# A norm's sums of squares as one row on TensorE instead of as columns

## The chip, the core and the metric

The kernel runs on one core of one Trainium2 chip. The core has five engines that matter here: TensorE (PE, with its weight loads shown apart as PEld), VectorE (DVE), ScalarE (ACT), GpSimd (POOL) and SyncE (SP), which issues most transfers. The metric is the device time of one execution in microseconds.

## The reference, cut to what matters

Four layers over a sequence of 256 tokens with 1024 features, batch 1: two with four mixers side by side, one hybrid, one of retention. Each layer has a mixer half and a feed-forward half. Each half begins with a norm of x; in the first two layers each half also ends with a norm of its output y:

```
def rms_norm(x, gain=None):
    y = xf * lax.rsqrt(jnp.mean(xf * xf, axis=-1, keepdims=True) + RMS_EPS)
...
h = rms_norm(x, norm_g[l, 0]) * (1.0 + sc1) + sh1
y = mixer_block(h, ...)
x = x + gt1 * rms_norm(y, norm_g[l, 1])
h = rms_norm(x, norm_g[l, 2]) * (1.0 + sc2) + sh2
y = jnp.square(jax.nn.relu(h @ w_up[l])) @ w_down[l]
x = x + gt2 * rms_norm(y, norm_g[l, 3])
```

In layers 2 and 3 the update is `x = x + gt * y` with no norm of y. So there are 8 norms of x and 4 norms of y, 12 in all.

## The kernel before

x is held transposed in SBUF, features on partitions: `X` is 128 x 8 x 256 (8 tiles `k` of 128 features, 256 tokens). The sum of squares of a token thus runs over partitions, and PE makes it: `unit_sums` (L586). The 8 tiles are grouped in five units, `UNITS = ((0, 1), (2, 3), (4, 5), (6,), (7,))`.

A norm of x (`norm_of`, L603) goes so. ACT squares a unit (L626) into one of two buffers `sq`, so that the Square of unit u waits until PE has summed unit u-2. PE multiplies the squares by a column of ones (L591). After the last unit ACT takes the root from PSUM (L629), DVE the reciprocal (L637), and `spread` (L599) lets PE broadcast the two columns `r` over all partitions as the row block `R` in PSUM. Then DVE multiplies a tile of X by R (L641), ACT adds the shift and rounds to `hi` (L632), DVE makes the remainder `lo` (L645), tile by tile, and the next projection (`gemm_phase`, L519) starts on the first tile of `hi`.

Weights come through a ring of six slots by DMA. Each slot is split by ACT into a rounded part (L411) and by DVE into a remainder (L417); PE multiplies three products of the parts. A slot is 48 matmul records of 128x256. The first slot of a phase is split ahead of the norm (`PRE = 1`), the second after it, since ACT and DVE run their instructions in the order of the code.

A norm of y stands in `rows_gemm_phase`. The last weight slot finishes the output tiles in the order of k. As each unit ends, ACT squares it from PSUM (L820) and takes a gated copy (L822), and PE puts the sums of a unit behind the multiplications (L789) of the next. Then follow root (L825), reciprocal (L844) and spread (L599), and DVE updates X unit by unit (L851, L853), which releases the Squares of the norm of x that follows. The order on each engine is that of the code, with semaphores between engines. A table load of ACT stands before the root where its last function was of another table.

A matmul with f32 operands shows as two records in the trace, each with its weight load. So a tile's two products with the column of ones are four records, each with a load of 128 columns of weights and one moving column.

Of the kernel before, what the change touches and what calls it, by code (L numbers as in the profile page):

```python
# [13 lines left out]
P = 128  # L14
SEQ = 256
# [230 lines left out]
def build(nc, stream, small, const, rows, x_in, pos_in, out, SM, CT):  # L246
    with ExitStack() as ctx:
# [42 lines left out]
        def cst(name):  # L290
            c, _, w = CT[name]
            return constS[:, c:c + w]
# [293 lines left out]
        def unit_sums(pe, u, sq, bank, ready, done):  # L586

            pe.wait_ge(*ready.at(u + 1))
            for c in range(len(UNITS[u])):
                for m in range(TT):  # L590
                    mm = pe.matmul(PS[:, bank, m:m + 1], sq[:, u % 2, c * SEQ + m * P:c * SEQ + (m + 1) * P], ones[:, 0:1],  # L591
                                   start=u + c + m == 0, stop=u == len(UNITS) - 1, skip_group_check=True)
            mm.then_inc(*done.one())

        def spread(pe, r, bank, ready, done):

            pe.wait_ge(*ready.at(1))
            for m in range(TT):
                mm = pe.matmul(PS[:, bank, m * P:(m + 1) * P], r[:, m:m + 1].to_broadcast((P, P)), ident, start=m == 0,  # L599
                               stop=True, skip_group_check=True)  # L600
            mm.then_inc(*done.one())

        def norm_of(l, half, updated):  # L603
# [3 lines left out]
            sq = area(TEMP_AT, 2, 512)  # L607
            tmp, r = spare[:, 0:1024].rearrange("p (i t) -> p i t", i=4), stat[:, 48:50]
            R = PS[:, 2, 0:SEQ]
            xsq, xsum, xrt, xr, rx, td, hd, ld = (sig(n) for n in (  # L610
                "x_squares", "x_square_sums", "x_roots", "x_rstd", "x_rstd_spread", "x_scaled", "h_hi_ready", "h_lo_ready"))
            state["h_hi"] = [hd.at(k + 1) for k in range(KD)]
            state["h_lo"] = [ld.at(k + 1) for k in range(KD)]

            def pe_part(pe):
                for u in range(len(UNITS)):
                    unit_sums(pe, u, sq, 0, xsq, xsum)
                spread(pe, r, 2, xr, rx)

            def act_part(act):  # L620
# [7 lines left out]
                act.wait_ge(*xsum.at(len(UNITS)))  # L628
                act.activation(r, PS[:, 0, 0:TT], ACT.Sqrt, bias=cst("eps"), scale=1.0 / D).then_inc(*xrt.one())  # L629
                for k in range(KD):  # L630
# [4 lines left out]
            def dve_part(dve):  # L635
                dve.wait_ge(*xrt.at(1))
                dve.reciprocal(r, r).then_inc(*xr.one())  # L637
                dve.wait_ge(*rx.at(1))
# [103 lines left out]
        def rows_gemm_phase(blk, name, l, lhs, half, acts_split=0, acts_ready=None, next_norm=None):  # L742
# [6 lines left out]
            gate = mod_part(l, half, 2)  # L749
            bd, ysq, ysum, yrt, yr, ry, yg, yt, xu = (sig(n) for n in (  # L750
                "tile_products", "y_squares", "y_square_sums", "y_roots", "y_rstd", "y_rstd_spread", "y_gated", "y_scaled", "x_updated"))
            following = slots_to_split() if next_norm else []
            norm = norm_of(*next_norm, xu) if next_norm else None
            sq, T, z = area(TEMP_AT, 2, 512), area(TEMP_AT + 1024, 2, 512), area(0, KD, SEQ)
            r, R = stat[:, 50:52], PS[:, 3, 0:SEQ]
            last, n_units = len(slots) - 1, len(UNITS)
# [17 lines left out]
            def _(pe):  # L774
# [23 lines left out]
                if normed:  # L798
                    unit_sums(pe, n_units - 1, sq, 0, ysq, ysum)
                    spread(pe, r, 3, yr, ry)  # L800
                if norm:
# [9 lines left out]
            def _(act):  # L811
                for n in slots[split_before:] + following:
                    split_hi(act, n)
                if normed:
# [9 lines left out]
                    act.wait_ge(*ysum.at(n_units))  # L824
                    act.activation(r, PS[:, 0, 0:TT], ACT.Sqrt, bias=cst("eps"), scale=1.0 / D).then_inc(*yrt.one())  # L825
                if norm:
# [3 lines left out]
            def _(dve):  # L830
# [11 lines left out]
                if normed:  # L842
                    dve.wait_ge(*yrt.at(1))
                    dve.reciprocal(r, r).then_inc(*yr.one())  # L844
                    dve.wait_ge(*ry.at(1))
# [95 lines left out]
        def short_mixers(l, convT, lqT, lkT, lrT, LV, LG, MU, MV, oT):  # L941
# [29 lines left out]
                "square_sums", "mean_ready", "root_ready", "outputs_ready", "outputs_turned", "gla_zeroed"))  # L971
            dfr, vn, wm, gt = sig("centred"), sig("gmlp_normed"), sig("ws_masked"), sig("gla_out_taken")
            c4 = c.rearrange("p (n t) -> p n t", n=4)
# [207 lines left out]
        def nsa_phase(l, kvcT, QK, VN, oT, S):  # L1181
# [21 lines left out]
            cs, sd, ex, pc = sig("cmp_scores"), sig("cmp_shifted"), sig("cmp_exp"), sig("cmp_probs")  # L1203
            pct, pcs, oc, oct_ = (sig(n) for n in ("cmp_probs_T", "cmp_probs_T_taken", "cmp_out", "cmp_out_taken"))
            ws, wt, mxd, pe_, ptp, pts, ob, obt = (sig(n) for n in (
                "scores_in_psum", "scores_taken", "row_max", "probs_ready", "probs_T_in_psum", "probs_T_taken",
                "attn_out", "attn_out_taken"))
            gd, fin, ft = sig("gates_ready"), sig("outputs_ready"), sig("outputs_turned")
# [403 lines left out]
        def delta_inputs(Q, AB):  # L1612
# [6 lines left out]
            taken = sig("gemm_bank_taken")  # L1619
            tap0, cv, sl, sqd, ss, rt, nr = (sig(n) for n in (  # L1620
                "first_tap", "conv_done", "conv_silu", "squares_ready", "l2_sums", "root_ready", "l2_done"))
            ga, ge, gl, bt = sig("gate_abs"), sig("gate_exp"), sig("gate_log"), sig("beta_ready")
# [569 lines left out]
```

## Time and profile before

| what | us |
|---|---|
| median of 3 runs | 1766.13 |
| lowest and highest of them | 1761.39, 1768.34 |
| the profiled execution's own time | 1766.4 |
| its span (first to last instruction) | 1764.4 |
| PE busy | 1561.6 |
| DVE busy | 1077.8 |
| ACT busy | 716.1 |

The span lies 2.0 us below the execution's own time. The mean granted TensorE clock over the span is 0.909 of full speed. A row of a timeline merges neighbouring instructions of one kind: it gives the start from the start of the span, the length, the engine, the line, what is written and read, the shape and the number of records, and in brackets how long the engine had been idle and who ended that. PEclk is the granted share of the TensorE clock: 1.00 is 2.4 GHz, 0.50 is 1.2 GHz.

### The profile page before, as it was taken

How to read it: one execution, taken by the hardware profiler on the slowest of the kernel's cores; microseconds unless marked ns; L12 is line 12 of the kernel's file. 1: busy time of each engine (PE TensorE's matmuls, PEld its weight loads, DVE VectorE, ACT ScalarE, POOL GpSimd, SP SyncE). 2: the span in 40 equal slices, each digit the busy share in tenths (PEclk: the TensorE clock that was granted, in tenths of full speed). 3: DMA queues.
4: the chain of work that ended last, by engine and by line, in shares of the span. 5: the costliest groups of instructions: out<-in, count | busy, mean ns of one | idle time of the engine just before them, and what ended most of it. 6: DMA issues, size and time to landing. Idle time of an engine off the chain costs nothing. (4 is left out here: it accounts for less than half of the span.)

```text
span 1764.4 us, 27370 instructions
## 1 busy us (share of the span) xinstructions
PE 1561.6 (89%) x11950; PEld 1506.8 (85%) x11950; DVE 1077.8 (61%) x1279; ACT 716.1 (41%) x797; POOL 277.4 (16%) x221
## 2 busy tenths in 40 slices
PE   2897689999898689999897685999989998899999
PEld 2886589999787589999897584999989997899998
DVE  6765757787455448688474633576895443456444
ACT  2533345433542445533474411433334443343332
POOL 0000200053000001044000111010253700300012
PEclk7998779999798579999798885899998999889999
DMA  9570549787140228888243001378893542436650
GB/s 395 224 262 1 207 187 350 291 332 291 72 160 32 76 92 320 324 308 333 99 170 117 1 1 35 146 281 303 312 354 144 189 173 93 143 129 229 217 211 29
DMA packets 47207, 336.71 MB, mean 191 GB/s; under 512 B 5360, under 2 KB 5744, under 8 KB 6768
## 3 DMA queue, kind: packets, MB, share of 16 engines
q1 hardware_dynamic: 46224, 333.09, 50.7%
q8 instruction: 94, 1.54, 0.3%
q10 hardware_dynamic: 864, 1.87, 0.3%
q14 instruction: 25, 0.20, 0.0%
HBM read 333.89 MB, written 1.05 MB: 190 GB/s over the span
## 5 line engine op out<-in xcount | busy, mean ns | idle before, releaser
L417 DVE TENSOR_TENSOR weights_hi_lo<-ring,weights_hi_lo 128x2048 fp32r<-128x2048 f32 x213 | 514.5, 2417 | 399.2 <-ACT weights_hi_lo L411 398.4
L411 ACT ACTIVATE weights_hi_lo<-ring 128x2048 fp32r<-128x2048 f32 x213 | 407.4, 1914 | 638.8 <-PE PS L519 347.1
L519 PE MATMUL PS<-hi,weights_hi_lo 128*128 128x256 f32 x3200 | 526.9, 288 | 25.5 <-DVE weights_hi_lo L417 17.1
L519 PEld LDWEIGHTS PS<-hi,weights_hi_lo 128*128 128x128 f32 x3200 | 451.3, 195 | 29.4 <-DVE weights_hi_lo L417 19.1
L789 PE MATMUL PS<-acts_hi_lo,weights_hi_lo 128*128 128x256 f32 x3552 | 446.3, 288 | 33.9 <-DVE weights_hi_lo L417 21.1
L789 PEld LDWEIGHTS PS<-acts_hi_lo,weights_hi_lo 128*128 128x128 f32 x3552 | 439.2, 196 | 41.3 <-DVE weights_hi_lo L417 25.0
L519 PE MATMUL PS<-lo,weights_hi_lo 128*128 128x256 f32 x1600 | 326.7, 286 | 0.0
L519 PEld LDWEIGHTS PS<-lo,weights_hi_lo 128*128 128x128 f32 x1600 | 253.8, 195 | 0.0
L428 DVE CUSTOM_DVE_ANT_0 ring<-ring,cond 128x1024 f32<-128x1024 f32 x192 | 248.4, 1333 | 1.0 <-DMA smallS<-in_small_dram 0.9
L737 POOL CAST acts_hi_lo<-arena 128x512 fp32r<-128x512 f32 x74 | 73.8, 998 | 993.6 <-PE PS L789 538.2
L519 PE MATMUL PS<-weights_hi_lo,hi 128*128 128x256 f32 x1248 | 203.2, 284 | 9.2 <-DVE weights_hi_lo L417 8.0
L519 PEld LDWEIGHTS PS<-weights_hi_lo,hi 128*128 128x128 f32 x1248 | 172.8, 190 | 12.0 <-DVE weights_hi_lo L417 9.0
L739 POOL TENSOR_TENSOR acts_hi_lo<-arena,acts_hi_lo 128x512 fp32r<-128x512 f32 x74 | 130.2, 1760 | 5.9
L519 PE MATMUL PS<-weights_hi_lo,lo 128*128 128x256 f32 x624 | 125.8, 283 | 0.0
L519 PEld LDWEIGHTS PS<-weights_hi_lo,lo 128*128 128x128 f32 x624 | 96.8, 189 | 0.0
L591 PEld LDWEIGHTS PS<-constS,arena 128*128 128x128 f32 x384 | 63.4, 256 | 23.1 <-ACT arena L626 22.2
L591 PE MATMUL PS<-constS,arena 128*128 128x1 f32 x384 | 64.0, 294 | 20.8 <-ACT arena L626 19.9
L400 PE MATMUL PS<-constS,arena 128*128 128x128 f32 x120 | 21.0, 338 | 37.0 <-DVE arena L1551 11.2
L400 PEld LDWEIGHTS PS<-constS,arena 128*128 128x128 f32 x120 | 17.8, 177 | 39.6 <-DVE arena L1551 11.4
L632 ACT ACTIVATE hi<-spare,mods 128x256 fp32r<-128x256 f32 x64 | 31.7, 506 | 31.8 <-DVE spare L641 31.8
L626 ACT ACTIVATE arena<-X 128x512 f32<-128x512 f32 (+1 forms) x40 | 21.7, 544 | 47.4 <-PE PS L591 18.7
L1955 POOL TENSOR_TENSOR arena<-arena,constS 128x1024 f32<-128x1024 f32 x6 | 11.9, 2000 | 181.4 <-DVE arena L1880 172.6
(325 smaller groups left out, 1100.4 us busy)
## 6 DMA issues: line engine op xcount, KB each, us to landing
ring<-in_stream_dram SPq DMA_DIRECT2D x313, 1024.0 KB, 4.9
constS<-in_const_dram SPq DMA_DIRECT2D x1, 1856.0 KB, 11.3
cond<-in_rows_dram SPq DMA_DIRECT2D x2, 512.0 KB, 6.0
arena<-in_x_dram ACTq DMA_DIRECT2D x1, 1024.0 KB, 12.5
smallS<-in_small_dram SPq DMA_DIRECT2D x1, 883.0 KB, 12.4
out_dram<-arena ACTq DMA_DIRECT2D x2, 256.0 KB, 2.5
out_dram<-arena SPq DMA_DIRECT2D x2, 256.0 KB, 2.9
constS<-in_const_dram SPq DMA_DIRECT2D x1, 320.0 KB, 13.0
```

The source lines that it names most:

```text
L400: mm = pe.transpose(PS[:, bank0 + i // 4, i % 4 * P:(i % 4 + 1) * P], src_of(i), ident)
L411: act.activation(wsp[:, g % 2, 0, :], ring[:, n % RING, :], ACT.Copy).then_inc(*hi_ready.one())
L417: dve.tensor_tensor(wsp[:, g % 2, 1, :], ring[:, n % RING, :], wsp[:, g % 2, 0, :].bitcast(F32), ALU.subtract).then_inc(used["dve"], 1)
L428: ins = dve.tensor_tensor_reduce(w[:, r, :], w[:, r, :], cond[:, 0 if q < 12 else 1, :], 1.0, 0.0, ALU.mult, ALU.add, mods[:, q, k:k + 1])
L519: mm = pe.matmul(o, lhs, rhs, start=k + g + j == 0, stop=k == KD - 1 and j == 2, skip_group_check=True)
L591: mm = pe.matmul(PS[:, bank, m:m + 1], sq[:, u % 2, c * SEQ + m * P:c * SEQ + (m + 1) * P], ones[:, 0:1], start=u + c + m == 0, stop=u == ...
L626: act.activation(sq[:, u % 2, 0:len(tiles) * SEQ], X[:, tiles[0]:tiles[-1] + 1, :].rearrange("p k t -> p (k t)"), ACT.Square).then_inc(*xs ...
L632: act.activation(hi[:, k, :], tmp[:, k % 4, :], ACT.Identity, bias=mods[:, q, k:k + 1]).then_inc(*hd.one())
L737: pool.tensor_copy(asp[:, a % 2, 0, :, :], src).then_inc(*acts_hi.one())
L739: pool.tensor_tensor(asp[:, a % 2, 1, :, :], src, asp[:, a % 2, 0, :, :].bitcast(F32), ALU.subtract).then_inc(*acts_lo.one())
L789: mm = pe.matmul(y_of(k), w[:, g, k * P:(k + 1) * P], x[:, g, :], start=i + g + j == 0 and (k % 2 == 0 or k == KD - 1), stop=i == last and ...
L1955: pool.tensor_tensor(CT[v % 2], LT, cst(f"level{v}").unsqueeze(1).broadcast_to((P, 8, P)), ALU.mult).then_inc(*ctd.one())
```

## The change

The squares become the moving operand and one column of ones the stationary one. A tile needs one matmul in place of two, with a single output partition: the sums of all 256 tokens form one row in PSUM. ACT takes the root of that row, 1x256 in place of 128x2, into a row of SBUF (`root`). Then PE turns the row into two columns with two matmuls of one contraction row each (new, in `spread`), and DVE takes the reciprocal of the columns from PSUM in place of SBUF. From there all is as before. A wait is added on PE (for the root) and the wait of the reciprocal is now for PE, not for ACT. All 12 norms use it. The rest of the diff drops names of semaphores that nothing used.

```diff
@@ -587,13 +587,17 @@
 
             pe.wait_ge(*ready.at(u + 1))
             for c in range(len(UNITS[u])):
-                for m in range(TT):
-                    mm = pe.matmul(PS[:, bank, m:m + 1], sq[:, u % 2, c * SEQ + m * P:c * SEQ + (m + 1) * P], ones[:, 0:1],
-                                   start=u + c + m == 0, stop=u == len(UNITS) - 1, skip_group_check=True)
+                mm = pe.matmul(PS[0:1, bank, 0:SEQ], ones[:, 0:1], sq[:, u % 2, c * SEQ:(c + 1) * SEQ],
+                               start=u + c == 0, stop=u == len(UNITS) - 1, skip_group_check=True)
             mm.then_inc(*done.one())
 
-        def spread(pe, r, bank, ready, done):
-
+        def spread(pe, root, r, bank, rooted, turned, ready, done):
+
+            pe.wait_ge(*rooted.at(1))
+            for m in range(TT):
+                mm = pe.matmul(PS[:, bank, SEQ + m:SEQ + m + 1], root[0:1, m * P:(m + 1) * P], ones[0:1, 0:1], start=m == 0, stop=True,
+                               skip_group_check=True)
+            mm.then_inc(*turned.one())
             pe.wait_ge(*ready.at(1))
             for m in range(TT):
                 mm = pe.matmul(PS[:, bank, m * P:(m + 1) * P], r[:, m:m + 1].to_broadcast((P, P)), ident, start=m == 0,
@@ -605,17 +609,17 @@
 
             q = mod_part(l, half, 0)
             sq = area(TEMP_AT, 2, 512)
-            tmp, r = spare[:, 0:1024].rearrange("p (i t) -> p i t", i=4), stat[:, 48:50]
+            tmp, r, root = spare[:, 0:1024].rearrange("p (i t) -> p i t", i=4), stat[:, 48:50], spare[0:1, 1024:1280]
             R = PS[:, 2, 0:SEQ]
-            xsq, xsum, xrt, xr, rx, td, hd, ld = (sig(n) for n in (
-                "x_squares", "x_square_sums", "x_roots", "x_rstd", "x_rstd_spread", "x_scaled", "h_hi_ready", "h_lo_ready"))
+            xsq, xsum, xrt, xc, xr, rx, td, hd, ld = (sig(n) for n in (
+                "x_squares", "x_square_sums", "x_roots", "x_roots_turned", "x_rstd", "x_rstd_spread", "x_scaled", "h_hi_ready", "h_lo_ready"))
             state["h_hi"] = [hd.at(k + 1) for k in range(KD)]
             state["h_lo"] = [ld.at(k + 1) for k in range(KD)]
 
             def pe_part(pe):
                 for u in range(len(UNITS)):
                     unit_sums(pe, u, sq, 0, xsq, xsum)
-                spread(pe, r, 2, xr, rx)
+                spread(pe, root, r, 2, xrt, xc, xr, rx)
 
             def act_part(act):
                 for u, tiles in enumerate(UNITS):
@@ -626,15 +630,15 @@
                     act.activation(sq[:, u % 2, 0:len(tiles) * SEQ],
                                    X[:, tiles[0]:tiles[-1] + 1, :].rearrange("p k t -> p (k t)"), ACT.Square).then_inc(*xsq.one())
                 act.wait_ge(*xsum.at(len(UNITS)))
-                act.activation(r, PS[:, 0, 0:TT], ACT.Sqrt, bias=cst("eps"), scale=1.0 / D).then_inc(*xrt.one())
+                act.activation(root, PS[0:1, 0, 0:SEQ], ACT.Sqrt, bias=cst("eps")[0:1], scale=1.0 / D).then_inc(*xrt.one())
                 for k in range(KD):
                     act.wait_ge(*td.at(k + 1))
                     act.activation(hi[:, k, :], tmp[:, k % 4, :], ACT.Identity,
                                    bias=mods[:, q, k:k + 1]).then_inc(*hd.one())
 
             def dve_part(dve):
-                dve.wait_ge(*xrt.at(1))
-                dve.reciprocal(r, r).then_inc(*xr.one())
+                dve.wait_ge(*xc.at(1))
+                dve.reciprocal(r, PS[:, 2, SEQ:SEQ + TT]).then_inc(*xr.one())
                 dve.wait_ge(*rx.at(1))
                 for k in range(KD + 1):
                     if k < KD:
@@ -747,12 +751,12 @@
             slots, todo = slots_of(name)
             normed = l < 2
             gate = mod_part(l, half, 2)
-            bd, ysq, ysum, yrt, yr, ry, yg, yt, xu = (sig(n) for n in (
-                "tile_products", "y_squares", "y_square_sums", "y_roots", "y_rstd", "y_rstd_spread", "y_gated", "y_scaled", "x_updated"))
+            bd, ysq, ysum, yrt, yc, yr, ry, yg, yt, xu = (sig(n) for n in (
+                "tile_products", "y_squares", "y_square_sums", "y_roots", "y_roots_turned", "y_rstd", "y_rstd_spread", "y_gated", "y_scaled", "x_updated"))
             following = slots_to_split() if next_norm else []
             norm = norm_of(*next_norm, xu) if next_norm else None
             sq, T, z = area(TEMP_AT, 2, 512), area(TEMP_AT + 1024, 2, 512), area(0, KD, SEQ)
-            r, R = stat[:, 50:52], PS[:, 3, 0:SEQ]
+            r, R, root = stat[:, 50:52], PS[:, 3, 0:SEQ], spare[0:1, 1280:1536]
             last, n_units = len(slots) - 1, len(UNITS)
             unit_ends = {tiles[-1]: u for u, tiles in enumerate(UNITS)}
 
@@ -797,7 +801,7 @@
                     mm.then_inc(*multiplied.one())
                 if normed:
                     unit_sums(pe, n_units - 1, sq, 0, ysq, ysum)
-                    spread(pe, r, 3, yr, ry)
+                    spread(pe, root, r, 3, yrt, yc, yr, ry)
                 if norm:
                     norm[0](pe)
 
@@ -822,7 +826,7 @@
                             ins = act.activation(z[:, k, :], y_of(k), ACT.Copy, scale=mods[:, gate, k:k + 1])
                         ins.then_inc(*yg.one())
                     act.wait_ge(*ysum.at(n_units))
-                    act.activation(r, PS[:, 0, 0:TT], ACT.Sqrt, bias=cst("eps"), scale=1.0 / D).then_inc(*yrt.one())
+                    act.activation(root, PS[0:1, 0, 0:SEQ], ACT.Sqrt, bias=cst("eps")[0:1], scale=1.0 / D).then_inc(*yrt.one())
                 if norm:
                     norm[1](act)
 
@@ -840,8 +844,8 @@
                 for n in following:
                     split_lo(dve, n)
                 if normed:
-                    dve.wait_ge(*yrt.at(1))
-                    dve.reciprocal(r, r).then_inc(*yr.one())
+                    dve.wait_ge(*yc.at(1))
+                    dve.reciprocal(r, PS[:, 3, SEQ:SEQ + TT]).then_inc(*yr.one())
                     dve.wait_ge(*ry.at(1))
                 for u, tiles in enumerate(UNITS):
                     n, ks = len(tiles), slice(tiles[0], tiles[-1] + 1)
...
```

PE at the end of the first y norm and the start of the x norm behind it (`y_squares`, `y_rstd` and `x_squares` are the semaphores waited for; L789 is the projection's own matmul), before:

```order
L591 MATMUL PS<-constS,arena 128x1 [waits y_squares]
L591 MATMUL PS<-constS,arena 128x1 x3
L789 MATMUL PS<-acts_hi_lo,weights_hi_lo 128x256 x6
L591 MATMUL PS<-constS,arena 128x1 [waits y_squares]
L591 MATMUL PS<-constS,arena 128x1
L591 MATMUL PS<-constS,arena 128x1 [waits y_squares]
L591 MATMUL PS<-constS,arena 128x1
L599 MATMUL PS<-constS,stat 128x128 [waits y_rstd]
L599 MATMUL PS<-constS,stat 128x128
L591 MATMUL PS<-constS,arena 128x1 [waits x_squares]
```

The same place on PE after the change (L590 are the sums, L598 the new turn, L603 the spread, L793 the projection):

```order
L590 MATMUL PS<-arena,constS 1x256 [waits y_squares]
L590 MATMUL PS<-arena,constS 1x256
L793 MATMUL PS<-acts_hi_lo,weights_hi_lo 128x256 x6
L590 MATMUL PS<-arena,constS 1x256 [waits y_squares] x2
L598 MATMUL PS<-constS,spare 128x1 [waits y_roots]
L598 MATMUL PS<-constS,spare 128x1
L603 MATMUL PS<-constS,stat 128x128 [waits y_rstd]
L603 MATMUL PS<-constS,stat 128x128
L590 MATMUL PS<-arena,constS 1x256 [waits x_squares]
```

Half as many matmuls make the sums, at the same places between the projection's, and two more stand between the root and the spread. On ACT and DVE no instruction is added, removed or moved; the root's shape and the reciprocal's source change. DVE at the same place, before and after:

```order
L417 TENSOR_TENSOR weights_hi_lo<-ring,weights_hi_lo 128x2048 [waits hi_ready]
L844 RECIPROCAL stat<-stat 128x2 [waits y_roots]
L851 TENSOR_TENSOR arena<-arena,PS 128x512 [waits y_gated,y_rstd_spread]
L853 TENSOR_TENSOR X<-X,arena 128x512 [waits y_scaled]
L851 TENSOR_TENSOR arena<-arena,PS 128x512 [waits y_gated]
```

```order
L417 TENSOR_TENSOR weights_hi_lo<-ring,weights_hi_lo 128x2048 [waits hi_ready]
L848 RECIPROCAL stat<-PS 128x2 [waits y_roots_turned]
L855 TENSOR_TENSOR arena<-arena,PS 128x512 [waits y_gated,y_rstd_spread]
L857 TENSOR_TENSOR X<-X,arena 128x512 [waits y_scaled]
L855 TENSOR_TENSOR arena<-arena,PS 128x512 [waits y_gated]
```

Nothing changes places there; the reciprocal waits one engine later.

## Rows read from the trace of the kernel before

**Rows 1.** The page's first line

```profile
span 1764.4 us, 27370 instructions
```

**Rows 2.** The chain that ended last, 1558 to 1695: start us, us, what

```profile
1558.26 2.90 PE PS L591 x24
...
1562.76 0.27 ACT stat L629
...
1563.27 1.24 PE PS L599 x4
...
1572.79 2.30 DVE weights_hi_lo L417
...
1575.13 119.88 PE PS L519 x1008
```

**Rows 3.** Timeline, 438 to 451: start us, us, instruction [idle before <-releaser]

```profile
438.79 0.26 ACT L825 ACTIVATE stat<-PS,constS 128x2 f32<-128x2 f32 x1 [0.33 <-PE PS L591]
...
440.05 0.69 DVE L851 TENSOR_TENSOR arena<-arena,PS 128x512 f32<-128x512 f32 x1 [0.80 <-PE PS L599]
...
442.18 6.98 PE L591 MATMUL PS<-constS,arena 128*128 128x1 f32 x32 [2.17 <-ACT arena L626]
...
445.27 0.42 DVE L853 TENSOR_TENSOR X<-X,arena 128x256 f32<-128x256 f32 x1
...
447.55 0.42 ACT L626 ACTIVATE arena<-X 128x256 f32<-128x256 f32 x1 [1.29 <-PE PS L591]
449.20 0.26 ACT L629 ACTIVATE stat<-PS,constS 128x2 f32<-128x2 f32 x1 [1.23 <-PE PS L591]
...
449.71 1.23 PE L599 MATMUL PS<-constS,stat 128*128 128x128 f32 x4 [0.55 <-DVE stat L637]
450.98 0.87 DVE L641 SCALAR_TENSOR_TENSOR spare<-X,mods,PS 128x256 f32<-128x256 f32 x2 [1.32 <-PE PS L599]
```

**Rows 4.** Windows: stretch, length, busy by engine, PEclk, DMA share, GB/s

```profile
33.00:40.20 7.20, 6.99 (x32) 6.90 (x32) 1.96 (x1) 3.32 (x6) 0.00 (x0) 0.50 1.01 420
43.10:49.30 6.20, 6.11 (x28) 6.14 (x29) 5.68 (x14) 4.26 (x8) 0.28 (x1) 0.50 0.75 302
...
442.10:449.20 7.10, 6.98 (x32) 6.90 (x32) 3.49 (x7) 2.12 (x6) 0.00 (x0) 0.50 0.00 1
452.10:455.60 3.50, 3.46 (x16) 3.49 (x17) 3.50 (x10) 2.11 (x5) 0.00 (x0) 0.51 0.00 0
...
143.20:148.30 5.10, 5.09 (x24) 4.23 (x25) 3.45 (x14) 0.11 (x1) 0.00 (x0) 0.50 0.01 3
1121.70:1124.60 2.90, 2.82 (x25) 2.82 (x25) 1.71 (x5) 1.71 (x4) 0.00 (x0) 0.99 0.79 322
```

**Rows 5.** Timeline of PE at 1484, dense f32 records of 512 columns

```profile
1484.50 10.46 PE L2085 MATMUL PS<-arena 128*128 128x512 f32 x24
```

**Rows 6.** Timeline of PE at 187, dense f32 records of 512 columns

```profile
187.51 3.78 PE L1464 MATMUL PS<-spare,constS 128*128 128x512 f32 x4 [2.98 <-DVE spare L1470]
```

**Rows 7.** Groups by form: count | busy us, mean ns | idle before

```profile
L645 DVE SCALAR_TENSOR_TENSOR lo<-spare,mods,hi 128x256 fp32r<-128x256 f32 x64 | 30.8, 481 | 2.9 <-ACT hi L632 2.9
L641 DVE SCALAR_TENSOR_TENSOR spare<-X,mods,PS 128x256 f32<-128x256 f32 x64 | 29.8, 476 | 10.5 <-PE PS L599 10.5
...
L1330 PE MATMUL PS<-ring,spare 128*32 128x128 f32 x128 | 18.3, 317 | 4.6 <-DVE spare L1227 4.6
...
L822 ACT ACTIVATE arena<-PS,mods 128x256 f32<-128x256 f32 x32 | 13.8, 473 | 0.0
...
L820 ACT ACTIVATE arena<-PS 128x256 f32<-128x256 f32 x8 | 3.1, 384 | 4.5 <-PE PS L789 4.5
...
L629 ACT ACT_TABLE_LOAD x2 | 2.6, 1283 | 0.0
```

**Rows 8.** Timeline at 849, DVE after a y norm's spread

```profile
849.51 0.69 DVE L851 TENSOR_TENSOR arena<-arena,PS 128x512 f32<-128x512 f32 x1 [1.31 <-PE PS L599]
```

**Rows 9.** Timeline at 1126, ACT at an x norm's root

```profile
1126.43 0.26 ACT L629 ACTIVATE stat<-PS,constS 128x2 f32<-128x2 f32 x1 [1.23 <-PE PS L591]
```

More of the change, by code:

```diff
@@ L971, in short_mixers @@
                 "square_sums", "mean_ready", "root_ready", "outputs_ready", "outputs_turned", "gla_zeroed"))
-            dfr, vn, wm, gt = sig("centred"), sig("gmlp_normed"), sig("ws_masked"), sig("gla_out_taken")
+            dfr, vn, wm = sig("centred"), sig("gmlp_normed"), sig("ws_masked")
             c4 = c.rearrange("p (n t) -> p n t", n=4)
@@ L1203, in nsa_phase @@
             cs, sd, ex, pc = sig("cmp_scores"), sig("cmp_shifted"), sig("cmp_exp"), sig("cmp_probs")
[L1204 to L1207, printed above, removed]
+            pct, pcs, oc = (sig(n) for n in ("cmp_probs_T", "cmp_probs_T_taken", "cmp_out"))
+            ws, wt, mxd, pe_, ptp, pts, ob = (sig(n) for n in (
+                "scores_in_psum", "scores_taken", "row_max", "probs_ready", "probs_T_in_psum", "probs_T_taken", "attn_out"))
             gd, fin, ft = sig("gates_ready"), sig("outputs_ready"), sig("outputs_turned")
@@ L1619, in delta_inputs @@
             taken = sig("gemm_bank_taken")
-            tap0, cv, sl, sqd, ss, rt, nr = (sig(n) for n in (
-                "first_tap", "conv_done", "conv_silu", "squares_ready", "l2_sums", "root_ready", "l2_done"))
+            tap0, cv, sl, sqd, ss, rt = (sig(n) for n in (
+                "first_tap", "conv_done", "conv_silu", "squares_ready", "l2_sums", "root_ready"))
             ga, ge, gl, bt = sig("gate_abs"), sig("gate_exp"), sig("gate_log"), sig("beta_ready")
```

## The prediction, made before the kernel ran

> **What bounds the kernel now.** I read the page first for the span [rows 1], then the chain that ended last, then a timeline of one norm, then windows for the granted clock. The chain is to be read from the bottom: nearly all of it is PE in the projections (119.88 us in one piece), and the pieces between are norms, in which it goes from engine to engine: PE's sums, the root 0.27, the spread 1.24, then DVE and ACT tile by tile and the split of the second weight slot on DVE, 2.30, before PE runs on [rows 2]. So a norm is serial and PE has nothing else to do in it; what a norm grows by, the span grows by, as long as PE is the bound behind it. I take that for all 12 norms.
>
> The timeline shows what a norm waits for [rows 3]. At 442.18 PE begins the sums of the x norm and is busy with them without a hole for 6.98 us, to 449.2. DVE has updated the last tile of X at 445.7, so for 3.5 us the sums alone hold the norm: ACT's Squares wait for PE (1.29 us before the last). Then the root comes 1.23 us after the last Square, the spread takes 1.32 us of DVE's time, and the projection starts. The windows say why the sums are slow: PEclk is 0.50 all through them, in this norm as in the first [rows 4]. At 1121.7 PE comes straight from a projection, at 2.4 GHz, and 25 of the same records take 2.82 us, 0.113 each, against 6.98/32 = 0.218.
>
> **The change, part by part.** Durations are from the profiled execution, 1766.4 us with a span of 1764.4, 0.3 us above the median of the runs shown.
>
> The sums. Before, a tile is four records, 0.87 us at 1.2 GHz and 0.45 at 2.4. After, it is one matmul with 256 moving columns, two records. Dense f32 records of 512 columns take (10.46 - 0.16)/24 = 0.429 us at 2.4 GHz [rows 5] and (3.78 - 0.2)/4 = 0.90 at 1.2 [rows 6], where I took off the last record's tail; half of that for 256 columns, twice for a tile: 0.43 and at most 0.90. So half as many matmuls are no less work: the weight load of 128 columns that paced a record is replaced by a stream of 256. At an equal clock the sums save (0.45 - 0.43) x 8 = 0.15 us in a norm of y, whose sums run at 2.4 GHz on PE's own path, 0.6 in four; in an x norm at 1.2 GHz I take nothing (0.87 against 0.85 to 0.90).
>
> The root. It reads 1x256 in place of 128x2. It is 0.26 now [rows 3]; ACT from PSUM with 256 columns and an operand of one column is 0.473, without that operand 0.384 [rows 7]. I take 0.47, since the root has such an operand: +0.21, bounds +0.12 and +0.25. That 127 partitions are left out saves nothing that a row shows. The Trainium skill (ScalarE: Activation LUTs, Rules for kernel authors) puts an instruction with a pointer bias at about 0.3 us plus 0.83 ns an element, an estimate of 0.51; by that the 12 roots cost 0.5 us more than by the row.
>
> The turn. Two matmuls, four records with one moving column, stand between root and reciprocal, with a hop on each side. The nearest row is the last unit's sums, the same four records between two ACT instructions: 1.23 us at 1.2 GHz [rows 3]. At 2.4 GHz it is the spread, 0.80 [rows 3], whose records have 128 moving columns. The hop from ACT to DVE falls away, 0.03. The reciprocal now reads PSUM: DVE with a PSUM operand takes 476 ns and without one 481 [rows 7], so nothing, at most 0.1. PE has nothing queued behind its new wait that could run before the spread, and DVE and ACT wait for that anyway: nothing covers the turn.
>
> So the fixed price of a norm is 0.21 + 1.23 - 0.03 = 1.41 us at 1.2 GHz and 0.21 + 0.80 - 0.03 = 0.98 at 2.4.
>
> The clock. This decides the rest. Through 7 us of records with one moving column, PE busy throughout, the clock stays at 0.50 [rows 4]. In projections behind a norm, records with 256 moving columns, it rises: 3.5 us after the start at 452.1 and 6.2 after that at 43.1, the shortest and longest of four such starts [rows 4]. It also rose 5.1 us into records whose stationary operand has only 32 columns, with 128 moving ones [rows 4, 7]. The new sums have one stationary column, fewer than any row, but stream 256 moving ones without a hole. I take it that they bring the clock up as the projections do.
>
> Then an x norm behind a y norm gains (6.98 - 3.5)/2 = 1.7 us at best and (6.98 - 6.2)/2 = 0.4 at worst in its sums, 1.1 in the middle; less 0.3, because at 2.4 GHz a Square that waits for PE (two buffers) leaves PE waiting in turn. I take 0.8. The turn and the spread follow within 3 us at 2.4 GHz: the spread's 1.32 becomes 0.80. Such a norm: 0.98 - 0.52 - 0.8 = -0.34, four of them -1.4. The first norm also has these sums, but a table load of 1.28 us [rows 7] stands behind its last Square and covers the end of them; I take 0. Two x norms of layers 2 and 3 come warm from a projection and lose the clock in the sums (1.23 us after the last Square, [rows 9], about 0.45 too much); if it holds: 0.98 - 0.52 - 0.45 = 0. The third has a table load there, which hid the sums: 0.98 - 0.52 = +0.46. The norms of y pay 0.98 x 4 = 3.9, less 0.6 for the sums; two of them had their spread at 1.2 GHz, as [rows 8], and I let one of these keep the clock: -0.5. Together +2.8.
>
> Nothing comes back at the start of the projection: the chain goes there over DVE to the second slot's split, not over PE's first slot [rows 2].
>
> The sum: -1.4 + 0 + 0 + 0.5 + 2.8 = +1.9, so 1768.3 us for the profiled kind of run, 1768 for the median.
>
> **The rivals.** (1) The new sums don't raise the clock. One stationary column of 128 may be too little work to count, and no row goes below 32. Then every x norm pays 1.41 (11.3 for eight), the y norms two at 0.98 and two at 1.41 less 0.6 (4.2): +15.5, 1782 us. Its place is the stretch from the first Square to the root; it decides wherever PEclk is 0.50 in the L590 stretch. The Trainium skill (TensorE: Matmul & The Clock Gate, Why this matters for your kernels) advises to keep TensorE busy continuously to reach the higher clock. By that the old sums, busy for 6.98 us, would have reached it too and the change could bring none: 12 x 0.98 - 0.6 = +11.2. The trace disagrees, 0.50 all through, so this reading gets no chance of its own.
>
> (2) The clock never falls between the y norm and the x norm, or is back at once. Then the x sums follow the Squares: the last tile of X at 445.7, its Square 0.12 later, 0.42 long, its sum 0.65 behind: 446.9 against 449.2, so 2.3 us a norm in place of 0.8, 6 us more in four, some 2 in the first norm: 1760 us. For it speaks that the y sums now stream too. Against it, PE does little from 438.8 to 442.2 but the spread, and will do little more [rows 3].
>
> (3) Small records don't run dense: the one-column weight load and a 256-column stream might leave holes of 0.1 us a record. 16 records in 12 norms would be up to 19 us where PE is the bound, some 12. The records with a 32-column load took 18.3 us for 128 of them, 0.14 each over both clocks [rows 7], with no hole of that kind, so I give this little; it ends near rival 1.
>
> **How the numbers follow.** The forecast has 0.66, its own range 1760 to 1775, since the clock's rise moves by 2.7 us between the rows and eight norms share it. Rival 1 has 0.23, rival 2 0.07, rival 3 0.04. A measurement of this kernel tells some 0.5% from no change, 8.8 us: faster is below 1757.3, slower above 1775. Faster gets 0.06 (most of rival 2 stays within), slower 0.27 (rivals 1 and 3), the same 0.67. The range for 8 in 10 takes in rival 1's middle: 1759 to 1783.
>
> **What would show it.** The L590 stretch of an x norm (32 records before, 16 after): PEclk well above 0.50 and 4.5 to 6.5 us long where I am right; 0.50 and 7 us in rival 1; under 5 with PEclk near 1 in rival 2. The root: 0.47 against 0.26. The gap of the reciprocal behind the root: 0.8 or 1.23. The spread's wait on DVE: 0.80 more often than 1.3. In the y norm's last slot the L590 records are 0.215 apart. I am wrong if the sums run at 1.2 GHz, or if the turn takes much more than 1.2 us.

## The result, and the profile after

| | median us (runs) | lowest to highest | profiled span | mean granted clock |
|---|---|---|---|---|
| before | 1764.71 (10) | 1760.09 to 1771.69 | 1764.4 | 0.909 |
| after | 1775.74 (10) | 1765.79 to 1782.22 | 1779.9 | 0.922 |

The ratio is 1.005, 95% between 1.0027 and 1.0072: some 8.8 us slower, and the whole interval lies above 1; the medians themselves lie 11.0 apart. The forecast was +1.9. The median after lies 0.7 us above the forecast's own range of 1760 to 1775 and inside its wider one of 1759 to 1783. The clock is higher on the mean, and the time is longer all the same; that is what has to be explained.

First the x norm of the forecast's rows, in the timeline (start us, us, instruction, idle before and releaser). They answer to [rows 3].

```profile
447.80 6.41 PE L590 MATMUL PS<-arena,constS 128*1 128x256 f32 x16 [2.17 <-ACT arena L630]
...
453.15 0.42 ACT L630 ACTIVATE arena<-X 128x256 f32<-128x256 f32 x1 [1.26 <-PE PS L590]
...
454.24 0.47 ACT L633 ACTIVATE spare<-PS,constS 1x256 f32<-1x256 f32 x1 [0.68 <-PE PS L590]
...
454.76 0.60 PE L598 MATMUL PS<-constS,spare 1*128 1x1 f32 x4 [0.56 <-ACT spare L633]
...
455.40 0.17 DVE L641 RECIPROCAL stat<-PS 128x2 f32<-128x2 f32 x1 [4.09 <-PE PS L598]
...
455.63 0.71 PE L603 MATMUL PS<-constS,stat 128*128 128x128 f32 x4 [0.26 <-DVE stat L641]
456.38 0.87 DVE L645 SCALAR_TENSOR_TENSOR spare<-X,mods,PS 128x256 f32<-128x256 f32 x2 [0.80 <-PE PS L603]
```

The sums take 6.41 us against 6.98, the root comes 0.68 us after the last Square against 1.23, the root is 0.47 against 0.26, the reciprocal starts 0.69 us after the root's end (454.71 to 455.40) against 0.03, and DVE waits 0.80 for the spread against 1.32. All of that was forecast, and the windows show why it is so: the clock rises in the sums. The columns are those of [rows 4]: the first norm, the x norm above, one that comes warm from a projection, where before the clock fell on the way [rows 9].

```profile
31.50:39.20 7.70, 5.52 (x16) 1.51 (x16) 2.78 (x5) 4.60 (x7) 0.00 (x0) 1.00 1.02 422
...
447.80:454.20 6.40, 6.27 (x16) 1.63 (x16) 3.41 (x7) 2.09 (x4) 0.00 (x0) 0.60 0.00 0
...
1131.90:1136.00 4.10, 3.85 (x16) 1.09 (x16) 1.68 (x5) 2.13 (x5) 0.00 (x0) 1.00 0.60 248
```

The 1.00 of the first row can't be taken as it stands. The first eight records of these sums (from 32.89 us) last 0.58 to 0.63 us and start 0.43 apart, twice the 0.22 of the later ones, which last 0.38: this is the pace of 1.2 GHz, whatever PEclk says there. The faster pace begins at about 36.5. So in the first norm, too, the clock rose within the sums.

The chain that ended last shows the same route as [rows 2], from the root over the turn and DVE to the split of the second weight slot (L417) and only then to PE:

```profile
1576.42 0.47 ACT spare L633
...
1576.94 0.61 PE PS L598 x4
...
1577.80 0.72 PE PS L603 x4
...
1586.80 2.30 DVE weights_hi_lo L417
...
1589.15 10.92 PE PS L519 x77
```

**Missed, first place: the sums inside the last weight slot of a y norm.** Here is PE's timeline there, first before, then after.

```profile
429.00 3.13 PE L789 MATMUL PS<-acts_hi_lo,weights_hi_lo 128*128 128x256 f32 x24 [0.38 <-DVE weights_hi_lo L417]
...
434.29 0.95 PE L591 MATMUL PS<-constS,arena 128*128 128x1 f32 x8
435.11 0.96 PE L789 MATMUL PS<-acts_hi_lo,weights_hi_lo 128*128 128x256 f32 x6
435.90 0.95 PE L591 MATMUL PS<-constS,arena 128*128 128x1 f32 x8
```

```profile
433.00 3.14 PE L793 MATMUL PS<-acts_hi_lo,weights_hi_lo 128*128 128x256 f32 x24 [0.39 <-DVE weights_hi_lo L417]
...
438.64 1.02 PE L590 MATMUL PS<-arena,constS 128*1 128x256 f32 x4
439.60 0.97 PE L793 MATMUL PS<-acts_hi_lo,weights_hi_lo 128*128 128x256 f32 x6
440.50 1.02 PE L590 MATMUL PS<-arena,constS 128*1 128x256 f32 x4
```

From one start of the sums to the next it is 434.29 to 435.90 = 1.61 us before and 438.64 to 440.50 = 1.86 after, with six records of the projection in both. From the slot's start to the root it is 438.79 - 429.00 = 9.79 before, and 443.54 - 433.00 = 10.54 after. In the weight loads' own rows an idle stretch stands before the first load of each return to the projection:

```profile
439.60 0.77 PEld L793 LDWEIGHTS PS<-acts_hi_lo,weights_hi_lo 128*128 128x128 f32 x6 [0.44 <-issue]
```

**Missed, second place: the second weight slot behind a norm.** PE's timeline at the third norm from the end, the last records of the first slot and the first of the second, before and after:

```profile
1137.28 0.40 PE L519 MATMUL PS<-lo,weights_hi_lo 128*128 128x256 f32 x2
1138.80 0.74 PE L519 MATMUL PS<-hi,weights_hi_lo 128*128 128x256 f32 x4 [1.13 <-DVE weights_hi_lo L417]
1139.38 0.40 PE L519 MATMUL PS<-lo,weights_hi_lo 128*128 128x256 f32 x2
1139.61 0.63 PE L519 MATMUL PS<-hi,weights_hi_lo 128*128 128x256 f32 x4
```

```profile
1146.14 0.40 PE L519 MATMUL PS<-lo,weights_hi_lo 128*128 128x256 f32 x2
1148.69 0.81 PE L519 MATMUL PS<-hi,weights_hi_lo 128*128 128x256 f32 x4 [2.15 <-DVE weights_hi_lo L417]
1149.31 0.64 PE L519 MATMUL PS<-lo,weights_hi_lo 128*128 128x256 f32 x2
1149.74 1.05 PE L519 MATMUL PS<-hi,weights_hi_lo 128*128 128x256 f32 x4
```

The clock rose 3.1 us after the first product, where before it took 5.4, so the first slot ended 1 us earlier against the split. PE waits 2.15 us for it in place of 1.13, the clock falls, and four records take 1.05 us where they took 0.63. The second slot is on the path, the first is not. The windows of 5.7 us from the start of the second slot, of before (three norms) and of after (five):

```profile
871.04:876.74 5.70, 5.70 (x35) 5.70 (x36) 2.29 (x1) 0.16 (x2) 0.00 (x0) 0.70 0.81 298
1138.80:1144.50 5.70, 5.70 (x48) 5.70 (x49) 4.44 (x5) 2.77 (x3) 0.00 (x0) 1.00 0.79 299
1575.13:1580.83 5.70, 5.70 (x48) 5.70 (x49) 2.29 (x1) 3.02 (x3) 0.00 (x0) 1.00 0.70 230
```

```profile
469.34:475.04 5.70, 5.70 (x33) 5.70 (x34) 2.14 (x1) 0.10 (x1) 0.00 (x0) 0.65 0.79 306
669.40:675.10 5.70, 5.70 (x48) 5.69 (x48) 5.70 (x5) 0.56 (x1) 3.07 (x2) 1.00 0.74 289
876.77:882.48 5.71, 5.71 (x26) 5.71 (x27) 2.15 (x1) 0.00 (x0) 0.00 (x0) 0.50 0.81 297
1148.69:1154.39 5.70, 5.70 (x35) 5.70 (x36) 4.44 (x5) 1.76 (x2) 0.00 (x0) 0.70 0.82 299
...
1589.15:1594.85 5.70, 5.70 (x35) 5.70 (x36) 2.15 (x1) 1.70 (x2) 0.00 (x0) 0.70 0.78 300
```

Of the eight norms in front of a projection, two had less than full clock there before (0.54 and 0.70) and four have it after. In 5.7 us PE gets 26 records done at 1.2 GHz all through, and 48 at 2.4 GHz.

The profiled span grew by 15.5 us, more than the medians. From the third weight split ahead of each x norm to the sixth behind it the eight stretches grew by 6.8 together: 2.7 up to the projection's first operand and 4.1 from there on. Of the 4.1, the two slots that are newly slow (1148.69 and 1589.15) make 3.1 and the one that went from 0.70 to 0.50 (876.77) makes 1.2. The other 8.7 lie outside the norms. The largest piece of it, 4.9 us, is a mixer of the first layer in which the clock fell in this execution and not in that of before. Before, then after:

```profile
174.09 5.54 PE L1394 MATMUL PS<-arena 128*128 128x64 f32 x48 [0.78 <-ACT arena L1431]
```

```profile
173.18 10.47 PE L1397 MATMUL PS<-arena 128*128 128x64 f32 x48 [1.09 <-ACT arena L1434]
```

That stretch took 5.54 us in six of the twelve profiles of this study (before and five variants), 8.69 in one and 10.47 in five, and the fastest but one kernel (1760.46 us) is among those with 10.47. I count it as the chance of one execution and not as the change's. So single spans are compared here only for how they are made up, and totals by medians and ratios.

### The profile page after: what moved, and what is told of

Its sections match the earlier page's. It is cut to its first block and busy times, and to the rows that moved or that the text cites. A ratio compares the mean times of both kernels' runs of the same rounds, so it can differ in the third digit from the quotient of the medians.

```text
span 1779.9 us, 27082 instructions
## 1 busy us (share of the span) xinstructions
PE 1565.9 (88%) x11806; PEld 1466.5 (82%) x11806; DVE 1075.9 (60%) x1279; ACT 718.4 (40%) x797; POOL 276.3 (16%) x221
## 3 DMA queue, kind: packets, MB, share of 16 engines
HBM read 333.89 MB, written 1.05 MB: 188 GB/s over the span
## 5 line engine op out<-in xcount | busy, mean ns | idle before, releaser
L417 DVE TENSOR_TENSOR weights_hi_lo<-ring,weights_hi_lo 128x2048 fp32r<-128x2048 f32 x213 | 514.1, 2416 | 404.9 <-ACT weights_hi_lo L411 403.9
L793 PEld LDWEIGHTS PS<-acts_hi_lo,weights_hi_lo 128*128 128x128 f32 x3552 | 439.8, 196 | 46.4 <-DVE weights_hi_lo L417 24.9
L519 PEld LDWEIGHTS PS<-hi,weights_hi_lo 128*128 128x128 f32 x3200 | 446.9, 194 | 36.8 <-DVE weights_hi_lo L417 27.1
L793 PE MATMUL PS<-acts_hi_lo,weights_hi_lo 128*128 128x256 f32 x3552 | 447.1, 288 | 33.8 <-DVE weights_hi_lo L417 21.0
L743 POOL TENSOR_TENSOR acts_hi_lo<-arena,acts_hi_lo 128x512 fp32r<-128x512 f32 x74 | 130.1, 1759 | 5.9
L590 PE MATMUL PS<-arena,constS 128*1 128x256 f32 x192 | 55.9, 431 | 21.3 <-ACT arena L630 20.1
L590 PEld LDWEIGHTS PS<-arena,constS 128*1 128x1 f32 x192 | 14.3, 90 | 54.8 <-ACT arena L630 32.3
L400 PEld LDWEIGHTS PS<-constS,arena 128*128 128x128 f32 x120 | 19.3, 188 | 39.6 <-DVE arena L1554 11.4
## 6 DMA issues: line engine op xcount, KB each, us to landing
smallS<-in_small_dram SPq DMA_DIRECT2D x1, 883.0 KB, 12.7
```

The costliest lines, as they stand in the source:

```text
L400: mm = pe.transpose(PS[:, bank0 + i // 4, i % 4 * P:(i % 4 + 1) * P], src_of(i), ident)
L417: dve.tensor_tensor(wsp[:, g % 2, 1, :], ring[:, n % RING, :], wsp[:, g % 2, 0, :].bitcast(F32), ALU.subtract).then_inc(used["dve"], 1)
L519: mm = pe.matmul(o, lhs, rhs, start=k + g + j == 0, stop=k == KD - 1 and j == 2, skip_group_check=True)
L590: mm = pe.matmul(PS[0:1, bank, 0:SEQ], ones[:, 0:1], sq[:, u % 2, c * SEQ:(c + 1) * SEQ], start=u + c == 0, stop=u == len(UNITS) - 1, skip ...
L743: pool.tensor_tensor(asp[:, a % 2, 1, :, :], src, asp[:, a % 2, 0, :, :].bitcast(F32), ALU.subtract).then_inc(*acts_lo.one())
L793: mm = pe.matmul(y_of(k), w[:, g, k * P:(k + 1) * P], x[:, g, :], start=i + g + j == 0 and (k % 2 == 0 or k == KD - 1), stop=i == last and ...
```

## The experiments

All were timed in five rounds against the kernel before, whose median was 1767.8 us, 1768.4 in the group of the last two. A ratio is to before.

**One half of the change at a time.** The x norms alone (the y norms keep their columns):

```diff
-                    unit_sums(pe, n_units - 1, sq, 0, ysq, ysum)
-                    spread(pe, root, r, 3, yrt, yc, yr, ry)
+                    unit_sums_cols(pe, n_units - 1, sq, 0, ysq, ysum)
+                    spread_cols(pe, r, 3, yr, ry)
```

> Only the 8 norms of x have the row form; the 4 norms of y keep columns. Theory A (from the trace after: in a y norm the last slot's sums grow by 0.72 us and root plus turn by 0.86, some 6.6 us in four; the x norms give back in their sums most of what root and turn cost): 0 to +3 us against the kernel before, 1765 to 1768. Theory B (the price is the root and the turn alone, 0.86 a norm in all twelve, the sums neither cost nor gain): +6.9 us, 1772.

Measured: 1771.41 (12 runs), ratio 1.002 [1.0006, 1.0034], +3.5 us, just above theory A and well below theory B. And the y norms alone, by the same edit in the x norm:

> Only the 4 norms of y have the row form. Theory A: +6 to +7 us, 1771 to 1772. Theory B: 4 x 0.86 = +3.4 us, 1768.5.

Measured: 1781.74 (7), ratio 1.0079 [1.0061, 1.0098], +13.9 us, above both theories. By the ratios the four y norms, where I had counted +2.8, cost the most, and the eight x norms a little. The two sum to 17.4, twice the change's 8.8. The halves may not be independent, since each shifts where the clock falls in the other; that wasn't shown. The profiled execution of the second took 1767.95 us and the other six 1778.25 to 1782.51, so its trace can't show what made the rest slow.

**The width of the stationary operand.** All 128 columns of the ones are loaded, and the sums come out in 128 partitions; root and turn read the first as before.

```diff
-                mm = pe.matmul(PS[0:1, bank, 0:SEQ], ones[:, 0:1], sq[:, u % 2, c * SEQ:(c + 1) * SEQ],
+                mm = pe.matmul(PS[:, bank, 0:SEQ], ones, sq[:, u % 2, c * SEQ:(c + 1) * SEQ],
```

> The changed kernel, but the sums use a stationary operand of 128 columns of ones in place of one, so that every PSUM partition holds the same row; the root still reads one partition, the turn and the spread stay. Theory A with its cause for the y norms (PE doesn't load the weights of a matmul with another number of columns ahead, so each change between the projection's 128 and the sums' 1 costs 0.1 to 0.2 us): the gaps before L590 and before the projection's records behind it go, the root of a y norm starts 0.7 us earlier in each, so 3 to 4 us below the changed kernel. Rival (the 0.72 us are the 256-column stream itself, or the waits for the Squares): the same as the changed kernel within 1 us.

Measured: 1777.21 (6), ratio 1.0057 [1.0038, 1.0077]: no gain in the total, where theory A had 3 to 4 us below the kernel after. But the trace shows what the width does to PE in the y norm:

```profile
429.93 3.14 PE L793 MATMUL PS<-acts_hi_lo,weights_hi_lo 128*128 128x256 f32 x24 [0.38 <-DVE weights_hi_lo L417]
...
435.19 1.02 PE L590 MATMUL PS<-arena,constS 128*128 128x256 f32 x4
435.87 1.06 PE L793 MATMUL PS<-acts_hi_lo,weights_hi_lo 128*128 128x256 f32 x6
436.76 1.02 PE L590 MATMUL PS<-arena,constS 128*128 128x256 f32 x4
```

```profile
439.71 0.47 ACT L829 ACTIVATE spare<-PS,constS 1x256 f32<-1x256 f32 x1 [0.43 <-PE PS L590]
```

From one start of the sums to the next 1.57 us, the 1.61 of before, and from the slot's start to the root 9.78, the 9.79 of before. So the 0.75 us were the switches between 128 and 1 stationary columns. Where this kernel lost it again is seen only in part: in its profile five of eight second slots start below full clock (0.50 to 0.70) in place of four, and in the three warm x norms the root comes 4.34, 4.76 and 4.34 us after the first sum, in place of 4.02, 4.65 and 4.02.

**No turn at all.** With 128 stationary columns the sums stand in every partition; the root and the reciprocal work on 128x256 and neither turn nor spread is needed.

```diff
-                act.activation(root, PS[0:1, 0, 0:SEQ], ACT.Sqrt, bias=cst("eps")[0:1], scale=1.0 / D).then_inc(*xrt.one())
+                act.activation(R, PS[:, 0, 0:SEQ], ACT.Sqrt, bias=cst("eps"), scale=1.0 / D).then_inc(*xrt.one())
...
-                dve.wait_ge(*xc.at(1))
-                dve.reciprocal(r, PS[:, 2, SEQ:SEQ + TT]).then_inc(*xr.one())
+                dve.wait_ge(*xrt.at(1))
+                dve.reciprocal(R, R).then_inc(*xr.one())
```

> The sums as in the wide form, with 128 columns of ones, and their row used as it is: root of 128x256, reciprocal of 128x256 into SBUF, no turn and no spread. If DVE takes a reciprocal at the rate of its other 128x256 operations (0.41 to 0.48 us), root plus reciprocal are 0.9 to 1.0 us in place of 0.26 + 0.17 + 0.22 + 0.80 to 1.32 before: 0.5 to 1.0 us less a norm, 6 to 11 us below the kernel before, 1754 to 1759. If the reciprocal needs several cycles an element (2 us or more), each norm is 0.5 us or more longer than before: 1771 or above. If the clock's return at the second weight slot takes 1.4 us a norm here too, the gain is halved.

Measured: 1773.43 (12), ratio 1.0035 [1.0018, 1.0051]. What the chain saves in hops, one instruction takes back:

```profile
448.67 0.47 ACT L631 ACTIVATE spare<-PS,constS 128x256 f32<-128x256 f32 x1 [0.79 <-PE PS L590]
449.18 1.75 DVE L639 RECIPROCAL spare<-spare 128x256 f32<-128x256 f32 x1 [3.77 <-ACT spare L631]
450.97 0.88 DVE L643 SCALAR_TENSOR_TENSOR spare<-X,mods,spare 128x256 f32<-128x256 f32 x2
```

From the root's start to DVE's next step it is 2.30 us, against 2.13 with the turn at 2.4 GHz (454.24 to 456.38 above, by their rounded starts 2.14).

**Keeping the clock in PE's wait for the second slot.** Two unused matmuls of 512 columns, 1.88 us of PE's time, into a PSUM bank that is free then, behind the first slot:

```diff
+                    if i == 0:
+                        for _ in range(2):
+                            pe.matmul(PS[:, 3, :], ident, X[:, 0:2, :], start=True, stop=True, skip_group_check=True)
```

On the kernel after:

> The changed kernel, with two f32 matmuls of 512 columns that nothing uses put on PE behind the first weight slot of each of the 8 projections after a norm of x (0.86 us each at 2.4 GHz), where PE waits for the second slot. Theory A (in the changed kernel the first slot runs at the higher clock, ends 1 us or more before its time of before, PE then sits idle for 2 to 3 us and the clock falls, so that the second slot, which is on the path, starts at 1.2 GHz and costs up to 1.7 us): the clock stays up, no second slot starts at 1.2 GHz, and the time falls 4 to 7 us below the changed kernel. Rival (the low clock at the second slot costs nothing, since DVE and ACT bound it, or falls at random): within 1 us of the changed kernel, or longer by the fill.

Measured: 1772.85 (9), ratio 1.0027 [1.0008, 1.0046], some 4 us less than after's 1.005. The two intervals overlap, so the total gives a direction; what the fill does to the clock is seen in the trace. On the kernel before:

> The kernel before with the same two matmuls behind the first slot. Theory A: there the first slot runs partly at 1.2 GHz and PE is idle for only 0.8 to 1.3 us before the second (4.4 and 1.9 in two cases), so the fill ends 0.5 to 0.9 us late in six cases and saves the clock in two: 0 to +4 us against the kernel before. Rival: the same gain as the fill brings in the changed kernel.

Measured: 1767.76 (12), ratio 1.0007 [0.9989, 1.0024]: no change. In the profiles, second slots at full clock are 7 of 8 and 8 of 8, where after had 4 and before 6. In the kernel before, whose waits are mostly about 1 us, the fill also makes three second slots start 0.2 to 0.4 us late. That this outweighs the two slots whose clock it kept isn't shown.

**128 moving columns without turning the sums.** The kernel before, its moving operand the ones' 128 columns in place of one; the root reads one column of each result. Nothing else is changed.

```diff
-                    mm = pe.matmul(PS[:, bank, m:m + 1], sq[:, u % 2, c * SEQ + m * P:c * SEQ + (m + 1) * P], ones[:, 0:1],
+                    mm = pe.matmul(PS[:, bank, m * P:(m + 1) * P], sq[:, u % 2, c * SEQ + m * P:c * SEQ + (m + 1) * P], ones,
```

> The kernel before, but the squares are multiplied by 128 columns of ones in place of one (the moving operand has 128 columns, the weight load that paces the record stays); the root reads one column of each block. No row, no turn, no change of the stationary operand's width. It does the clock's part of the change alone. Theory A: PEclk rises within the sums of the x norms as in the changed kernel (L591 of an x norm 5 to 6 us long against 7), the y norms' last slot is as before, so 0.7 to 1.0 us less up to the projection in five x norms; at the second slot up to 1.4 us a norm goes back where the first slot now runs at 2.4 GHz. Together 1760 to 1768, within 4 us of the kernel before and 8 to 12 us below the changed kernel. Theory B (the clock rises for the stream of 256 columns behind one stationary column only, or not at all): the same as before within noise, with PEclk 0.50 in L591.

Measured: 1768.98 (12), ratio 1.0004 [0.9988, 1.002]. The clock rises in the sums and the turn isn't paid, and still nothing is gained. Up to the projection time is won: all twelve spreads run at 2.4 GHz, and from the root's start to DVE's next step it is 15.1 us over the twelve norms against 20.3. It goes at the second slots. The last norm shows PE's wait there, and the same norm with the fill (L524) behind the first slot shows it filled. PE's timeline, without the fill and with it:

```profile
1562.09 4.37 PE L591 MATMUL PS<-constS,arena 128*128 128x128 f32 x32
1567.02 0.71 PE L599 MATMUL PS<-constS,stat 128*128 128x128 f32 x4 [0.55 <-DVE stat L637]
...
1578.37 0.75 PE L519 MATMUL PS<-hi,weights_hi_lo 128*128 128x256 f32 x4 [3.07 <-DVE weights_hi_lo L417]
```

```profile
1560.28 4.38 PE L594 MATMUL PS<-constS,arena 128*128 128x128 f32 x32
...
1574.31 1.88 PE L524 MATMUL PS<-X,constS 128*128 128x512 f32 x4
1576.55 0.75 PE L519 MATMUL PS<-hi,weights_hi_lo 128*128 128x256 f32 x4 [0.36 <-DVE weights_hi_lo L417]
```

At this one norm the clock held in both, in spite of 3.07 us; at seven of the eight it was below full without the fill, at one with it. The kernel with 128 columns and the fill:

> The 128-column form with the two unused matmuls behind the first slot of each projection. Theory A: it keeps both the gain in the sums and the clock at the second slot: 6 to 10 us below the kernel before, 1757 to 1761. If the loss at the second slot is not the clock's, no better than the 128-column form alone.

Measured: 1760.46 (12), ratio 0.9955 [0.9934, 0.9975], 8 us faster than before and the first to gain. Neither part brings anything alone (1.0004 and 1.0007); together they do. The interval lies clear of that of the 128 columns alone, [0.9988, 1.002], and the kernels differ by the fill only: this is the firmest evidence that the clock at the second slot costs time.

**The best version.** Unused matmuls also behind the y norm's spread (4) and the x norm's (2), each of 256 columns:

```diff
+                    for _ in range(4):
+                        pe.matmul(PS[:, 2, 0:SEQ], ident, constS[:, 0:256], start=True, stop=True, skip_group_check=True)
```

> The 128-column form with the unused matmuls behind the first slot, and more of them where PE waits in a norm: 1.7 us worth (at 2.4 GHz) behind the spread of a y norm, 0.9 behind the spread of an x norm. If the clock is what the sums of an x norm still pay for (L594 takes 5 to 6.5 us behind a y norm against 4.4 where PE comes from a projection), the clock stays up from the y norm on, those sums take 4 to 5 us, and the time is 2 to 5 us below the form with one fill, 1756 to 1759. If the fills delay the Squares' sums or the first product instead, it is the same or longer.

Measured: 1755.02 (6), ratio 0.992 [0.9889, 0.995]: 14 us faster than before, faster than both kernels. Its interval overlaps that of the kernel with one fill by a little, so the 14 us are firm and the share of the added fills is less so. The x norm's sums now run at 2.4 GHz (PEclk 1.00 from 438.9 to 444.1):

```profile
436.64 1.89 PE L807 MATMUL PS<-constS 128*128 128x256 f32 x8
438.97 1.16 PE L594 MATMUL PS<-constS,arena 128*128 128x128 f32 x8 [0.44 <-ACT arena L631]
440.29 1.16 PE L594 MATMUL PS<-constS,arena 128*128 128x128 f32 x8 [0.17 <-ACT arena L631]
441.62 2.44 PE L594 MATMUL PS<-constS,arena 128*128 128x128 f32 x16 [0.17 <-ACT arena L631]
```

Their 6.98 us are 5.09 (438.97 to 444.06), and PE waits for the Squares and no longer they for PE: rival 2 of the forecast, brought about on purpose.

**The turn by itself.** The wide kernel with the fill differs from 128 columns with the fill by the row's root and the turn, and also by the sums: 16 records of 256 moving columns in place of 32 of 128, which in the profiles bring the root of each y norm and of each warm x norm about 0.1 us earlier.

> The row form with 128 columns of ones stationary and the unused matmuls behind the first slot: it differs from the 128-column form with the same fill only in the row's root (0.465 against 0.262) and the turn (0.66 more between root and reciprocal), 0.86 us a norm. If all that was argued on the sums and the clock holds and nothing else is in it, 12 x 0.86 = 10 us above that form, 1770 to 1772. If the turn is partly covered, less than 6 us above.

Measured: 1767.93 (12), ratio 1.0002 [0.9982, 1.0022]. Against 0.9955 that is 0.47% or 8.3 us in twelve norms, 0.69 each, where 0.86 was expected; with the two intervals' widths the 8.3 may be 3 to 13. Against the kernel after with the fill (1.0027) it is 0.25% or 4.4 us, for the width, where 3.0 were counted in the trace for the four y norms; these two intervals overlap, so this one is a direction only.

## Why the prediction held in its wider range and missed in its steps

- **The clock in the sums: right.** Behind the four y norms PEclk is 0.60 to 0.75 over the sums, where it was 0.50; in the three x norms that come warm from a projection it is 1.00, where it was 0.80 to 0.89. Rival 1 is refuted. The stretch from the first sum to the root became shorter by 0.6 to 1.8 us behind the four y norms, 1.3 on the mean, where I had taken 0.8 of a middle of 1.1.
- **Root, turn, reciprocal: right.** 0.466 against 0.47 taken; 0.66 more between root and reciprocal where 0.77 was taken at 2.4 GHz; the reciprocal from PSUM 0.171 against 0.166 from SBUF. The Trainium skill (ScalarE: Activation LUTs, Rules for kernel authors) gives an estimate of 0.51 for the root; the trace has 0.466. Over twelve norms the stretch from the root's start to DVE's next step grew from 20.3 to 27.1 us, 0.57 a norm.
- **The sums of y: failed.** The step "at an equal clock the sums save (0.45 - 0.43) x 8 = 0.15 us in a norm of y" was read from dense rows of one shape. It left out the change of shape: in the last slot PE goes four times from the projection's 128 stationary columns to one and three times back, and the root comes 0.75 us later (9.79 to 10.54; 0.78, 0.76, 0.75 and 0.71 in the four). That is +3.0 where -0.6 stood. Rival 3 looked for holes inside a run of these records; they are at its ends. The Trainium skill (TensorE: Matmul & The Clock Gate, Step-by-step: what each phase is for) says that PE pulls a weight load ahead of matmuls in flight; the trace agrees while the width stays (1.57 and 1.61 us a round) and shows 0.44 us without a load at the return where it changes.
- **The start of the projection: failed, and the larger miss.** "Nothing comes back at the start of the projection" was true of the time won in the first slot, and I stopped there. I did not ask what PE does with it: it waits 2.15 us in place of 1.13, the clock falls, and the second slot, which is on the path, starts at 1.2 GHz in four norms of eight in place of two. In the profile this is 4.1 us. The fill takes some 4 us out of the ratio (1.005 to 1.0027, in overlapping intervals), and some 9 us, clear of noise, on the kernel with 128 columns, where seven slots were slow (1.0004 to 0.9955).

The forecast's terms beside what the profile has of them, up to the projection's first operand:

| term | forecast | measured |
|---|---|---|
| sums of four y norms | -0.6 | +3.0 |
| root, turn and spread of four y norms | +3.4 | +3.7 |
| sums of four x norms behind them | -3.2 | -5.1 |
| root, turn and spread of these | +1.8 | +1.4 |
| first x norm, two warm ones, one with a table load | 0, 0, 0, +0.5 | -0.7, -0.3, -0.1, +0.8 |
| sum | +1.9 | +2.7 |
| from there on, above all the second slots | 0 | +4.1 |

So up to the projection +3.6 on the sums of y stood against -1.9 on those of x and -1.1 on the first and the two warm norms, and the sum came out right by luck. The median stayed inside the wider range because that range had been drawn for rival 1, which did not come about. The norms together are 6.8 us by the profile, against 8.8 by the ratio with an interval of 4.8 to 12.7.

Open: why the y norms alone cost more (13.9) than the whole change; and whether the mixer of the first layer keeps or loses its clock by chance or by something ahead of it. No run here tells.

## What to carry to other kernels

A stretch that is off the path still sets whether the engine behind it is kept at its clock: when PE gets faster in front of a wait, look at the wait's length and at the granted clock behind it before anything is booked as neutral. Price a matmul where it stands, between its neighbours; here a stationary operand of another width cost at the changes of it, not in the row that shows it dense. And here the clock was had without turning the reduction, by widening a moving operand whose record was paced by the weight load, together with unused matmuls where PE waits; neither gained anything alone.

## What the runs showed of the hardware

- The clock rose while PE ran records with one stationary column and 256 moving ones (PEclk 0.60 over the 6.4 us at 447.80), and with 128 stationary and 128 moving ones (0.57 over the 6.8 us at 444.65 of the kernel with 128 columns). Over 7 us of records with one moving column it stayed at 0.50.
- PEclk can read 1.00 where PE runs at 1.2 GHz: in the first norm after the change its records start 0.43 us apart until 36.3 us. The spacing of equal records tells.
- With 128 moving columns in place of one, 32 records take 4.37 us; at 2.4 GHz 25 records with one moving column took 2.82 [rows 4], 3.6 for 32. In a warm x norm it is a matter of the clock which is longer: at 1121.78 before, with the clock falling on the way, the 32 with one moving column took 4.61; at 1332.05 of the kernel before with the fill, where the clock held, they took 3.95, and those with 128 took 4.27 in the same norm (at 1331.12).
- A reciprocal of 128x256 on DVE takes 1.75 us, of 128x2 0.17; the norms' other DVE instructions of 128x256 take 0.42 to 0.48.
- A wait of some 2 us on PE may cost the clock or not: at 1358.62 of the kernel after it held behind a wait of 1.39, at 669.40 behind 3.08, and at 1148.69 it fell behind 2.15.
